# Feed-forwards of a two-block transformer in fp32r pairs: two of seven half products take high and low input in one 512-column pass

## What is computed

```python
def swiglu_ffn(x, w_up, w_down):
    gate, up = jnp.split(x @ w_up, 2, axis=-1)
    return (jax.nn.silu(gate) * up) @ w_down
...
        h = h + swiglu_ffn(rmsnorm(h, norm_ffn[l]), ffn_w_up[l], ffn_w_down[l])
```

## Time and profile before

| | |
|---|---|
| median of 3 runs | 1570.14 us |
| profiled execution | 1571.84 us |
| its span | 1570.1 us |
| TensorE busy | 1539.3 us, 98% |
| VectorE busy | 1136.1 us, 72% |
| ScalarE busy | 882.8 us, 56% |
| GpSimd busy | 887.6 us, 57% |
| share of the chain that ended last, TensorE | 71% |

### The profile page before, as it was taken

One profiled execution on the slowest core, in us unless ns is written; L12 is line 12 of the kernel. 1 busy time (PEld: TensorE's weight loads), 2 busy tenths in 40 slices (PEclk: granted clock), 3 DMA queues, 4 the chain that ended last, 5 costly groups with the idle time before them and its releaser, 6 DMA issues.

```text
span 1570.1 us, 28469 instructions
## 1 busy us (share of the span) xinstructions
PE 1539.3 (98%) x10794; PEld 1371.8 (87%) x10794; DVE 1136.1 (72%) x1788; ACT 882.8 (56%) x1482; POOL 887.6 (57%) x523
## 2 busy tenths in 40 slices
PE   6999999999999999999999999999999999999997
PEld 4888888888888778578999999988788999999996
DVE  7887597687687869987766766764666766776755
ACT  4555355355355645567664665554667666566553
POOL 1444445445335448837777777654215677677653
PEclk8999999999999999999999999999999999999999
DMA  9422322322322456712333333353112333333332
GB/s 374 148 81 95 121 79 96 111 77 94 120 80 85 141 98 163 197 54 93 108 108 108 108 100 103 108 174 97 55 51 68 108 99 103 108 103 99 108 121 68
DMA packets 53660, 173.12 MB, mean 110 GB/s; under 512 B 5404, under 2 KB 11581, under 8 KB 53053
## 3 DMA queue, kind: packets, MB, share of 16 engines
q1 hardware_dynamic: 47296, 159.90, 32.1%
q10 hardware_dynamic: 6268, 11.95, 3.3%
HBM read 165.48 MB, written 6.36 MB: 109 GB/s over the span
## 4 chain that ended last, share of the span: by engine, by line
PE 71%; DVE 3%; issue 2%; POOL 2%; ACT 2%; DVEq 0%; ACTq 0%; POOLq 0%
PE gps L2651 8%; PE gps L2650 8%; PE gps L2649 8%; PE gps L2209 7%; PE gps L2211 7%; PE gps L2210 7%; PE aps L2649 4%; PE aps L2651 4%; PE aps L2650 4%; PE gps L2570 2%; POOL w_lo L678 1%; PE gps L2267 1%; PE gps L2268 1%; PE gps L2269 1%; PE aps L2739 1%
## 5 line engine op out<-in xcount | busy, mean ns | idle before, releaser
L678 POOL TENSOR_TENSOR w_lo<-w_raw,w_hi 128x1024 fp32r<-128x1024 f32 x140 | 363.8, 2603 | 466.5 <-ACT w_hi L804 466.3
L2209 PE MATMUL gps<-xa_hi,w_hi 128*128 128x512 f32 x639 | 256.7, 402 | 2.5 <-DVE xa_lo L1502 2.5
L2211 PE MATMUL gps<-xa_hi,w_lo 128*128 128x512 f32 x639 | 250.2, 392 | 0.0
L2210 PE MATMUL gps<-xa_lo,w_hi 128*128 128x512 f32 x639 | 250.2, 392 | 0.0
L804 ACT CAST w_hi<-w_raw 128x1024 fp32r<-128x1024 f32 x140 | 146.3, 1045 | 96.8 <-DMA w_raw<-weights_dram 42.3
L2209 PEld LDWEIGHTS gps<-xa_hi,w_hi 128*128 128x128 f32 x639 | 120.5, 189 | 30.4 <-DVE xa_lo L1502 4.1
L2211 PEld LDWEIGHTS gps<-xa_hi,w_lo 128*128 128x128 f32 x639 | 120.6, 189 | 26.2
L759 POOL TENSOR_TENSOR w_lo<-diff,w_hi 128x512 fp32r<-128x512 f32 x60 | 77.6, 1294 | 113.0 <-ACT w_hi L1151 113.0
L2210 PEld LDWEIGHTS gps<-xa_lo,w_hi 128*128 128x128 f32 x639 | 120.7, 189 | 22.6
L1913 DVE TENSOR_TENSOR sums<-aps,sums 128x512 fp32r<-128x512 f32 x58 | 40.1, 692 | 135.6 <-ACT sums L1145 135.6
L753 POOL TENSOR_TENSOR w_lo<-w_raw,w_hi 128x512 fp32r<-128x512 f32 x60 | 94.0, 1567 | 34.0 <-ACT w_hi L1128 34.0
(11 more groups left out here) (505 smaller groups left out, 5118.9 us busy)
## 6 DMA issues: line engine op xcount, KB each, us to landing
w_raw<-weights_dram SPq DMA_DIRECT2D x268, 512.0 KB, 3.6
ada_w<-ada_in_dram SPq DMA_DIRECT2D x8, 1024.0 KB, 18.7
gates<-ret_tab_dram ACTq DMA_DIRECT2D x4, 1024.0 KB, 6.5
spread<-glu_scratch_dram SPq DMA_DIRECT2D x12, 270.0 KB, 4.6
rel_scratch_dram<-rel_rows ACTq DMA_DIRECT2D x1, 3072.0 KB, 34.6
x<-x_turned_dram SPq DMA_DIRECT2D x2, 1024.0 KB, 7.5
res<-xT_dram ACTq DMA_DIRECT2D x1, 2048.0 KB, 10.5
bias<-rel_scratch_dram ACTq DMA_DIRECT2D x1, 2048.0 KB, 8.6
```

Of the source, the lines that this page charges most:

```text
L678: TT(w_lo[:, j, :], w_raw[:, j, :], w_hi[:, j, :].bitcast(F32), ALU.subtract).then_inc(lo_ready[j], 1)
L2209: mm(gps[:, j, :], w_hi[:, j, w], x[0][:, k, :], start=k == 0, stop=False)
L2210: mm(gps[:, j, :], w_hi[:, j, w], x[1][:, k, :], start=False, stop=False)
L2211: last = mm(gps[:, j, :], w_lo[:, j, w], x[0][:, k, :], start=False, stop=k == blocks - 1)
```

## The change

In rounds 2 to 29 of each feed-forward, `diff` and `w22` write into a whole PSUM bank (`WIDE_SUM[s]`, 512 columns). One pass multiplies the high weights with high input and low input side by side; the high part lands in the bank's first half, where it landed before, and the product with the low input in the second. The third pass (low weights, high input) stays as it is. The second half has then to be added: ScalarE copies it behind `diff` into `low_copy[s]` (a new instruction behind step 2), and VectorE adds in `wide_lows` this copy to `UP_ROW[s]` and the final second half to the copied row in `hbuf`. Both adds stand at the head of `gate_and_up` and of `down_added`. Rounds 0 and 1 stay as they were (`PLAIN_PAIRS`). Four semaphores elsewhere in the kernel are merged into others to make room for the three new ones.

```diff
+        WIDE_SUM = (aps[:, 2, :], gps[:, 2, :])
...
+        low_copy = [lnv[:, s * TH:(s + 1) * TH] for s in range(2)]
+        PLAIN_PAIRS = 2
...
                     copied(f, 2, hbuf[:, 2 * s + 1, TH:], UP_SUM[s])
+                    if n >= PLAIN_PAIRS:
+                        if wide_at(layer, n) > 1:
+                            act.wait_ge(low_added, wide_at(layer, n) - 1)
+                        nc.scalar.copy(low_copy[s], WIDE_SUM[s][:, TH:]).then_inc(low_copied, 1)
...
+                def wide_lows(n):
+
+                    f, s = f0 + n, n % 2
+                    if n < PLAIN_PAIRS:
+                        return
+                    dve.wait_ge(low_copied, wide_at(layer, n) + 1)
+                    dve.wait_ge(partial_copied, 4 * f + 4)
+                    TT(UP_ROW[s], UP_ROW[s], low_copy[s], ALU.add).then_inc(low_added, 1)
+                    dve.wait_ge(sum_full, wide_at(layer, n) + 1)
+                    row = hbuf[:, 2 * s + 1, 0:TH]
+                    own.mark(TT(row, WIDE_SUM[s][:, TH:], row, ALU.add))
+                    dve.wait_ge(low_added, wide_at(layer, n) + 1)
+                    own.wait()
+
                 def gate_and_up(n, part, k):
 
                     f, I, s = f0 + n, up + n // 2, n % 2
+                    wide_lows(n)
...
                 def down_added(n, m):
 
                     I, s = up + n // 2, n % 2
+                    wide_lows(n)
...
-            def seven_products(f, I, s, x, lead=None, mixes=None):
+            def seven_products(f, I, s, x, lead=None, mixes=None, wide=True):
...
-                def product(name, out, start=False, k0=0, k1=HALF):
+                pair_high = slice(0, 2)
+
+                def product(name, out, start=False, k0=0, k1=HALF, wide_out=None):
 
                     more = {} if start else {"skip_group_check": True}
                     for k in range(k0, k1):
@@ -2646,11 +2675,15 @@
                         if mixes is not None and name == "diff":
                             pe.wait_ge(hid_mix_low, mixes + k + 1)
                         w = slice(k * P, (k + 1) * P)
-                        mm(out, highs[s][name][:, w], x[name](k, 0), start=start and k == 0, stop=not start, **more)
-                        mm(out, highs[s][name][:, w], x[name](k, 1), start=False, stop=not start, **more)
+                        if wide_out is not None:
+                            mm(halves(wide_out), highs[s][name][:, w], x[name](k, pair_high), start=start and k == 0, stop=not start, **more)
+                        else:
+                            mm(out, highs[s][name][:, w], x[name](k, 0), start=start and k == 0, stop=not start, **more)
+                            mm(out, highs[s][name][:, w], x[name](k, 1), start=False, stop=not start, **more)
                         last = mm(out, lows[s][name][:, w], x[name](k, 0), start=False, stop=not start or k == HALF - 1, **more)
...
+                two = WIDE_SUM[s] if wide else None
...
-                last = product("diff", UP_SUM[s], start=True, k1=split)
+                last = product("diff", UP_SUM[s], start=True, k1=split, wide_out=two)
...
-                    product("diff", UP_SUM[s], start=True, k0=split).then_inc(product_done, 1)
+                    product("diff", UP_SUM[s], start=True, k0=split, wide_out=two).then_inc(product_done, 1)
...
-                product("w22", UP_SUM[s])
+                last = product("w22", UP_SUM[s], wide_out=two)
+                if wide:
+                    last.then_inc(sum_full, 1)
...
-                seven_products(f0, up, 0, x, lead=layer_n)
+                seven_products(f0, up, 0, x, lead=layer_n, wide=False)
```

More of the change, by code:

```diff
@@ L451, in program @@
         partial_copied = sem("partial_copied")
+        low_copied = sem("low_copied")
+        low_added = sem("low_added")
+        sum_full = sem("sum_full")
         scaled = sem("scaled")
@@ L576, in copies_at, with wide_at @@
             return layer * (FF_MIXES + 1) + (FF_STARTS[part] + k) // 2
+        def wide_at(layer, n):
+            return layer * (FF_PAIRS - PLAIN_PAIRS) + n - PLAIN_PAIRS
         def mixes_before(layer, part):
@@ L1060, in _ @@
             nc.scalar.preload_act_table(ACT.Sigmoid)
-            act.wait_ge(bias_ready, 1)
+            act.wait_ge(bias_ready, 2)
             for c in range(KC):
@@ L1110, in _ @@
             act.wait_ge(mean_small, 1)
-            nc.scalar.activation(small[:, 3, :], small[:, 0, :], ACT.Square).then_inc(mean_square, 1)
+            nc.scalar.activation(small[:, 3, :], small[:, 0, :], ACT.Square).then_inc(mean_small, 1)
             act.wait_ge(mean_rows, 1)
-            nc.scalar.copy(by_tile(mean_wide), rows_of).then_inc(mean_copied, 1)
+            nc.scalar.copy(by_tile(mean_wide), rows_of).then_inc(mean_rows, 1)
             act.wait_ge(var_ready, 2)
@@ L1857, in _ @@
             dve.wait_ge(both_ready, 1)
-            dve.wait_ge(bias_ready, 1)
+            dve.wait_ge(bias_ready, 2)
             for c in range(KC):
@@ L1872, in _ @@
             taps(TAP_PLAN[KC - 1][part_end:])
-            dve.wait_ge(mean_square, 1)
+            dve.wait_ge(mean_small, 2)
             dve.wait_ge(sum_done, SUMS[RMS_LN])
@@ L1878, in _ @@
             TS(small[:, 1, :], small[:, 1, :], 0.0, None, ALU.max).then_inc(var_ready, 1)
-            dve.wait_ge(mean_copied, 1)
+            dve.wait_ge(mean_rows, 2)
             dve.wait_ge(x_ready, KC * X_PW2)
@@ L2538, in _ @@
             mm(aps[0:AH, 3, 0:REACH + 1], rel[:], hot[:], start=True, stop=True).then_inc(rel_full, 1)
-            mm(aps[:, 2, 0:KC], ones[:], vec[:, VEC["b_dw"]:VEC["b_dw"] + KC], start=True, stop=True).then_inc(bias_parts, 1)
+            mm(aps[:, 2, 0:KC], ones[:], vec[:, VEC["b_dw"]:VEC["b_dw"] + KC], start=True, stop=True).then_inc(bias_ready, 1)
             layer_then("pw1", KC // 2, xb, x_wait(X_CONV_IN), lambda: sum_running(RMS_FIRST, double=True))
@@ L2604, in _ @@
             keep_busy(6)
-            pe.wait_ge(mean_copied, 1)
+            pe.wait_ge(mean_rows, 2)
             pe.wait_ge(rstd_small, 1)
@@ L2693, in quads @@
                             seven_products(i * 2 + (f0 + s), i + up, s, x)
-                seven_products(f0, up, 0, x, lead=layer_n)
+                seven_products(f0, up, 0, x, lead=layer_n, wide=False)
                 pe.wait_ge(evicted[1], up + 1)
                 sum_running(norm, bank=NORM_BANK, last_square=SQUARES[KC - 1])
-                seven_products(f0 + 1, up, 1, x)
+                seven_products(f0 + 1, up, 1, x, wide=False)
                 at = 1
```

5 lines of the change are left out of this document (1 added, 4 removed).

## The result

The changed kernel takes 1582.93 us (median of 6 runs, 1580.06 to 1584.88), the kernel before, beside it, 1570.84 us (6 runs, 1568.38 to 1572.36). The ratio is 1.0075, 95% interval 1.0065 to 1.0085: slower by 12.1 us. The forecast was +7.1 us, 1577.2: the measured time lies above the forecast's own range (1575 to 1582) and 0.07 us inside the wider one (1569 to 1583). The profiled execution has a span of 1580.4 us, 10.3 more than before.

The account below looks back on a forecast made before the run. TensorE, busy 98% of the span, was taken to bound the kernel. New waiting of 13.1 us minus 6.0 us of passes gave +7.1 us, a median of 1577.2 us; own range 1575 to 1582, wider 1569 to 1583.

Parts of the forecast that it names:

- The mechanism: Adds ahead of gate times rstd delay silu and first copy; TensorE waits at `sum2` in 36 rounds, 13.1 us together.
- Hidden and faster: Rival: the wait at `sum2` stays hidden and the kernel gains 6.0 us, 1564.1 us; chance 0.12.
- the third copy late too: Rival: the copy `sum1` waits for comes late, 0.2 us in 12 rounds, +2.4 us, 1579.6 us; chance 0.07.
- Its cover: Room for the third copy before `sum1`, counted from the first copy's start: chain 3.24 us, `sum1` after 3.46 us.
- Merge worth nothing: Rival: alternating wide and narrow passes on TensorE save nothing, +9.2 us, 1579.3 us; chance 0.05.
- D: Delay of gate times rstd by VectorE's two adds ahead of it: 0.83 us, between 0.77 and 0.96.
- The slack: Delay the chain can take before TensorE waits at `sum2`: 0.49 us in loops, 0.55 outside, 0.21 in four rounds.
- The allowance of 0.22 for the restart: After a late first copy, `sum2` on TensorE behaves as if begun 0.22 us after that copy's end.
- The merge: Two narrow TensorE passes become one wide in `diff` and `w22`: 0.0133 us saved each, 6.0 us in all.
- The periods forecast: Round lengths in the changed profile: an "up" round 10.3 us, a "down" round 9.97 us.
- The sum: Over both layers, 13.1 us of new waiting minus 6.0 us of passes: +7.1 us.
- VectorE's two adds delay only results that are due a round later: In "down" rounds the adds were costed at nothing; these 16 rounds gain their 0.107 us.

Follow-up runs that it names:

- e1: Changed kernel with both adds moved behind gate times rstd in "up" rounds: 1569.57 us, ratio 0.9997 to the kernel before.
- e5: Changed kernel with the first add moved into VectorE's wait ahead of the last sum's low part, the second left ahead of the gate: 1568.95 us, ratio 0.9987.
- e6: Changed kernel with the first add ahead of the last sum's low part and the second behind gate times rstd: 1568.03 us, ratio 0.9980.
- e7: Changed kernel with a third add of the same size, into a buffer nothing reads afterwards, ahead of gate times rstd: 1591.99 us, ratio 1.0129.
- e3: Changed kernel without VectorE's two adds, keeping the wide passes and ScalarE's copy, so the result is incomplete: 1566.97 us, ratio 0.9981.
- e2: Changed kernel with wide passes alone, without ScalarE's copy and VectorE's two adds, so the result is incomplete: 1565.93 us, ratio 0.9969.
- e8: Changed kernel without the two adds in "down" rounds, so their low part is missing from the result: 1576.81 us, ratio 1.0035.
- e4: Changed kernel with the narrow passes of before, keeping ScalarE's copy and VectorE's two adds, so the result differs: 1582.76 us, ratio 1.0080.

## Why the prediction was right, and by how much it was short

**The mechanism** was right: two adds ahead of gate times rstd, the first copy late, TensorE waiting at `sum2` in 36 rounds; e1, e5, e6 and e7 show it from four sides. "Hidden and faster" fell with the first timeline, "the third copy late too" with e3, where the copy costs nothing. Its cover was thinner than counted: the second copy starts 1.38 behind the first (902.86, 904.24 in the earlier trace rows) and not 0.27 + 1.02, so that the chain is 3.33 of 3.46 us and not 3.24. "Merge worth nothing", whose 1579.3 lies nearer to the result than the forecast, fell with e2.

**D** was forecast at 0.83 and measured 0.83 (0.84 from the cast).

**The slack** was forecast at 0.49 in a loop. Delays of 0.51, 0.84 and 1.11 (e5, the changed kernel, e7, each against e1) give waits of 0.00, 0.26 and 0.54 (the interval's change plus the 0.07 that the passes give): a line with slope 1 and a threshold of 0.57. Three delays of another origin fit it: in e1 the gate is 1.31 late at interval 15 and 2.42 late at 18, in e3 1.30 at 7, and the waits are 0.72, 1.84 and 0.72. The step was mis-sized by 0.08, in two parts. The passes bring `sum2` only 0.06 nearer to the cast (5.23 us in e1, 898.21 to 903.44; before 5.29, 898.75 to 904.04), not 0.107. And the copy doesn't move by the whole of D: from the start of gate times rstd to its start are 1.31 us before (901.55, 902.86), 1.28 in e1 and 1.26 in the changed kernel (904.08, 905.34); why is open. The allowance of 0.22 for the restart was right: in the changed kernel the copy ends at 905.71 and the second pass starts at 906.06, as if `sum2` had begun at 905.94. Waits: 0.26 instead of 0.34 in 28 rounds, 0.19 instead of 0.28 in four, about 0.56 instead of 0.62 in four: 10.3 us instead of 13.1.

**The merge** was forecast at 0.0133 each, and gave 0.0084 (0.067 a round over 8 merges; e2: 3.5 us over the intervals from 4 on, and nothing before, where TensorE waits for other things), because a wide pass between narrow ones holds 0.2346 and not 0.2267, while the narrow one between two wide holds 0.1169 instead of 0.12 (means over 436 and 378 in the changed kernel): 0.3515 for the pair, in the place of 0.36. By the formula of the Trainium skill, "TensorE: Matmul & The Clock Gate", section Back-to-back issue gap, which is given there for an isolated matmul, a merge saves 2.5 ns; that is about as far off on the other side. The periods forecast were 10.3 and 9.97; they are 10.28 and 10.01.

**The sum** of these two errors is near zero: 10.3 - 3.5 = 6.8 us against 7.1, and e8 and the layers' sums without the odd intervals measure 6.8 and 6.7. It came out right by luck, because both terms were too large by about the same amount, 2.8 and 2.5.

**What fell short** is the sentence that in "down" rounds "VectorE's two adds delay only results that are due a round later". True of the results, but not of the operations behind them: two that read two SBUF operands fell behind a GpSimd operation. This gave 2 x 1.3 us at interval 15. The 2.4 us at interval 18 of layer 1 come from the late start and not from the adds, and no reading of the order could have given them. 6.8 + 2.6 + 2.4 = 11.8, beside the measured +12.1. So the time stayed inside the wider range, by 0.07 us, but it had no term for these 5 us; the upper part of the range stood for a larger D (0.96 gives +11.8).

Two smaller statements were inexact. The earlier trace rows has TensorE's only wait for one of ScalarE's copies; the same view lists waits for ScalarE outside the feed-forwards (L2327, 1.2 us). And three semaphores, not four, were merged elsewhere.

## What to carry to other kernels

Work put on an engine with 25% idle time cost 13 us or nothing by its place alone: find the chain that the next wait ends on, put added operations into a wait that is there already or behind the last operation of that chain, and give the slack of every link before believing that something fits. A view of waits lists only what shows as idle time; on TensorE look also for a first pass that is longer and starts later than its like. Where a VectorE operation with two SBUF operands and a GpSimd operation lie close together, look at who starts first, at each place that the change shifts: 0.16 us was all that kept a 0.70 us operation from becoming a 1.39 us one.

## What was not expected of the hardware

- A VectorE operation with two SBUF operands that starts behind a GpSimd one takes 1.39 to 1.44 us instead of 0.42 or 0.70, and 2.77 behind one of 2.40. One start earlier it is GpSimd's that is longer, 1.69 instead of 1.28, which nobody waited for here.
- A VectorE operation can start 0.35 us late with nothing in the profile that holds it, at a place that moves with the length of its stream; thirteen such starts were found, each with a packet of queue q14 within 3 us behind. Those at L1907 cost time, as the operation fell behind a GpSimd one; the others cost nothing. The one at 1401 us of the changed kernel cost 2.4 us, and is absent with sixteen idle instructions at the start of the stream.
- After a wait of 2.4 us TensorE's clock fell once (e4: 0.79 in the mean of 8 us, 1.5 us lost), and after the same wait in the changed kernel it did not.
- A pass of 512 columns started 0.2346 us ahead of the next in turn with passes of 256 (which then held 0.1169 instead of 0.12), 0.2325 in a row of four, and 0.2267 in a long row of its own kind.
